# First-level scores of a gated recurrence as biased exponentials, and four reordered stage openings

## The reference

```python
# output projections, three times for the 2048 tokens (8 feature tiles in, 16 in the last)
y = jnp.concatenate([...], axis=-1) @ w_out[l]
x = x + gate[:, None, :] * y
# gated recurrence, per chunk, 4 heads of width 128
cum = jnp.cumsum(li, axis=2)
diff = cum[:, :, :, None, :] - cum[:, :, None, :, :]
decay = jnp.where(causal, jnp.exp(jnp.where(causal, diff, 0.0)), 0.0)
scores = jnp.einsum('bhtd,bhsd,bhtsd->bhts', qi, ki, decay)
```

## Time and profile before

| | us |
|---|---|
| median of 3 executions | 4637.68 |
| lowest, highest | 4636.55, 4641.71 |
| profiled execution, its own time | 4641.9 |
| its span in the trace | 4640.2 |
| mean granted clock of TensorE | 0.926 |

### The profile page before, as it was taken

How to read it: one execution, slowest core, us unless ns; L and a number is a source line. 1 busy time by engine, 2 the same in 40 slices (tenths; PEclk the granted TensorE clock), 3 DMA queues, 4 the chain that set the end, 5 groups by cost and what they waited for, 6 DMA issues and landing times. The chain is left out here.

```text
span 4640.2 us, 51312 instructions
## 1 busy us (share of the span) xinstructions
PE 3943.1 (85%) x19136; PEld 3222.7 (69%) x19136; DVE 2494.6 (54%) x3386; ACT 1577.0 (34%) x2597; POOL 1140.8 (25%) x972
## 2 busy tenths in 40 slices
PE   4659998798895999869879799999997968776998
PEld 1548887686574888668758578878885656664776
DVE  2645943687363594368736643330000489994554
ACT  2332102675211210257622212241111755553331
POOL 1421110121111111012111111111110158874443
PEclk7879999799997999889989899999998989997999
DMA  5341112322454112232246412131211465554443
GB/s 214 120 152 63 68 77 88 96 64 81 155 199 144 71 75 77 78 97 64 62 154 231 162 68 77 72 141 68 81 68 68 136 155 146 147 136 158 171 169 111
DMA packets 315680, 529.46 MB, mean 114 GB/s; under 512 B 26806, under 2 KB 203574, under 8 KB 299512
## 3 DMA queue, kind: packets, MB, share of 16 engines
q1 hardware_dynamic: 276874, 353.84, 24.6%
q0 software_dynamic: 38592, 172.82, 10.0%
HBM read 373.57 MB, written 153.00 MB: 113 GB/s over the span
## 5 line engine op out<-in xcount | busy, mean ns | idle before, releaser
L450 PE MATMUL in_ps<-h,in_wp 128*128 128x512 f32 x6624 | 1510.3, 390 | 18.6 <-POOL in_wp L613 18.6
L450 PEld LDWEIGHTS in_ps<-h,in_wp 128*128 128x128 f32 x6624 | 1247.6, 188 | 281.4 <-POOL in_wp L613 21.6
L1656 PE MATMUL out_ps<-out_y,out_wp 128*128 128x512 f32 x3072 | 728.5, 399 | 77.0 <-ACT out_y L1536 34.5
L1656 PEld LDWEIGHTS out_ps<-out_y,out_wp 128*128 128x128 f32 x3072 | 589.1, 192 | 216.3 <-issue 65.7
L583 DVE SCALAR_TENSOR_TENSOR cy<-cu,in_cw,cy 128x2048 f32<-128x2048 f32 x120 | 314.5, 2621 | 4.3
L872 PE MATMUL att_O<-att_pT,att_vs 128*128 128x512 f32 x960 | 302.8, 424 | 0.0
L1589 POOL TENSOR_TENSOR out_wp<-out_w,out_wp 128x2048 fp32r<-128x2048 f32 (+1 forms) x48 | 192.7, 4016 | 441.7 <-ACT out_wp L1525 441.6
L511 ACT ACTIVATE in_ob<-in_ps 128x2048 f32<-128x2048 f32 x37 | 69.7, 1885 | 664.1 <-PE in_ps L450 664.1
L613 POOL TENSOR_TENSOR in_wp<-in_w,in_wp 128x1024 fp32r<-128x1024 f32 x75 | 201.6, 2690 | 250.3 <-ACT in_wp L461 214.6
L992 DVE TENSOR_TENSOR att_pT<-att_T,att_pT 128x512 fp32r<-128x512 f32 x320 | 219.6, 686 | 73.8 <-ACT att_pT L925 65.7
L1918 DVE TENSOR_SCALAR hi_z<-hi_z 128x4 f32<-128x4 f32 x1 | 0.2, 172 | 462.0 <-ACT hi_z L1875 462.0
...
## 6 DMA issues: line engine op xcount, KB each, us to landing
...
```

Source lines behind the costliest of these rows:

```text
L450: mm = nc.tensor.matmul(ps[:, q, c * W:(c + 1) * W], wp[:, q, i, k], h[:, j, k, c * W:(c + 1) * W], start=(n + k == 0), stop=(n == 2 and k ...
L1656: mm = nc.tensor.matmul(ps[:, u % NB, :W], wp[:, u % NW, a, k], y[:, c % 2, b, k], start=(i + k == 0), stop=(i == 2 and k == KY - 1))
```

## The change

Four stage functions are edited.

1. `project`, only where there are decays (`in_2`): the weight parts of tiles (0,0), (0,1) and (1,0) are all made ahead of the first body, the last of them on ACT after the input heads.
2. `attention`: the queries of block 0 are loaded and rounded ahead of the second piece of keys; the rests of the first pieces stand ahead of the constants on DVE; the value parts and the later key pieces, which stood behind the eight heads of block 0, stand between them.
3. `project_out`. In `out` of the first layer: two buffers `mw`, and the unused products go to PSUM (two banks, for which the units' banks fall from 5 to 4); in both layers `gather` comes ahead of `modulation`, and each dot product waits for the one before. In `out_2`: the second weights are loaded and rounded right behind the first input piece; PE takes units 0 and 1 piece by piece (`pieces`, 12 matmuls for each piece) and no longer one after the other; in chunks 1 to 3 the squares of units 0, 1 and 2 are taken together in the place of the third.
4. `mixers`: level 0 has no differences. DVE writes the negated sum at the middle of the chunk (`edge`, 128x4), and ACT takes the exponentials straight from `hc` and `hkc` with a bias for each head: 8 of 128x64 in the place of one of 128x512. `pick(c, 0)` copies the one quarter of `psL` that level 0 fills (64 partitions by 4x64).

```diff
+        soon = decays
         def tiles(eng, body, ahead=None, only=None):
             def tile(it, q, *rest, last=False):
-                if ahead is not None and not last:
+                if ahead is not None and not last and not (soon and isinstance(it, int) and it == 0):
                     ahead(it + q, 1 - q)
                 body(rest[0], it, q, *rest[1:])
             if ahead is not None:
                 ahead(0, 0)
+                if soon:
+                    ahead(0, 1)
+                    ahead(1, 0)
...
+                if soon and isinstance(it, int) and (it, q) == (1, 0):
+                    heads()
...
-            for p in range(FIRST):
+            keys(0)
+            queries(0)
+            for p in range(1, FIRST):
                 keys(p)
...
+            def value_heads(g):
+                act.wait_ge(v_in, 32 if win else 16)
+                nc.scalar.activation(vs[:, :, 0, 2 * g * HD:(2 * g + 1) * HD], vf[:, :, g * HD:(g + 1) * HD], ACT.Copy).then_inc(vled, 1)
-            for p in range(FIRST):
-                key_heads(p)
+            key_heads(0)
             query_heads(0, 0)
             query_heads(0, 1)
+            for p in range(1, FIRST):
+                key_heads(p)
             for hh in range(NH):
                 exps(0, hh)
                 if hh < 2:
                     query_heads(1, hh)
+                elif hh < 4:
+                    value_heads(hh - 2)
+                elif FIRST + hh - 4 < len(cuts):
+                    key_heads(FIRST + hh - 4)
             sink_exps(0)
-            act.wait_ge(v_in, 32 if win else 16)
-            for g in range(2):
-                nc.scalar.activation(vs[:, :, 0, 2 * g * HD:(2 * g + 1) * HD], vf[:, :, g * HD:(g + 1) * HD], ACT.Copy).then_inc(vled, 1)
-            for p in range(FIRST, len(cuts)):
-                key_heads(p)
...
+            def value_rest(g):
+                dve.wait_ge(vled, g + 1)
+                of, to = slice(g * HD, (g + 1) * HD), slice(2 * g * HD, (2 * g + 1) * HD)
+                tt(vs[:, :, 1, to], vf[:, :, of], vs[:, :, 0, to].bitcast(F32), ALU.subtract).then_inc(vparted, 1)
+            for p in range(FIRST):
+                key_rest(p)
...
                 maxima(0, hh)
+                if 3 <= hh < 5:
+                    value_rest(hh - 3)
+                elif 5 <= hh and FIRST + hh - 5 < len(cuts):
+                    key_rest(FIRST + hh - 5)
             shift(0)
-            dve.wait_ge(vled, 2)
-            for g in range(2):
-                of, to = slice(g * HD, (g + 1) * HD), slice(2 * g * HD, (2 * g + 1) * HD)
-                tt(vs[:, :, 1, to], vf[:, :, of], vs[:, :, 0, to].bitcast(F32), ALU.subtract).then_inc(vparted, 1)
-            for p in range(FIRST, len(cuts)):
-                key_rest(p)
...
-    NB, SQ, S1, S2 = 5, 5, 6, 7
+    NB, SQ, S1, S2 = (4, 4, 5, None) if later and not middle else (5, 5, 6, 7)
...
+    FIRST, SQUARE_AT = (G, 0) if kept else (1, 2)
...
+        products = s.ps("products", [P, 2 * CH]) if later and not middle else None
...
-                wait(sp, dotted, j * m_n)
-                sp.dma_start(mw[:], m_w[j]).then_inc(mw_in, 16)
+                wait(sp, dotted, (j + 1 - NMW) * m_n)
+                sp.dma_start(mw[:, j % NMW], m_w[j]).then_inc(mw_in[j % NMW], 16)
...
-            weights(1)
+                if p + 1 == FIRST:
+                    weights(1)
...
-                square(u)
+                if kept or c == 0 or n > SQUARE_AT:
+                    square(u)
+                elif n == SQUARE_AT:
+                    for v in range(u - SQUARE_AT, u + 1):
+                        square(v)
...
+            def pieces():
+                for p in range(G):
+                    for u in range(2):
+                        for i, (a, b) in enumerate(PARTS):
+                            if p == 0 and i < 2:
+                                pe.wait_ge((led, parted)[i], u + 1)
+                            if u == 0 and i != 1:
+                                pe.wait_ge((yled, None, yparted)[i], p + 1)
+                            for k in range(p * KP, (p + 1) * KP):
+                                mm = nc.tensor.matmul(ps[:, u, :W], wp[:, u, a, k], y[:, 0, b, k], start=(i + k == 0), stop=(i == 2 and k == KY - 1))
+                        if p == G - 1:
+                            mm.then_inc(mm_done, 1)
             pe.wait_ge(const, 3 if middle else 2)
-            for u in range(U):
+            if not kept:
+                pieces()
+            for u in range(0 if kept else 2, U):
...
-                dve.wait_ge(mw_in, 16 * (j + 1))
+                dve.wait_ge(mw_in[j % NMW], 16 * (j // NMW + 1))
                 dve.wait_ge(silued, m_n)
                 for n in range(m_n):
-                    out = unused if n + 1 < m_n else mw
-                    nc.vector.tensor_tensor_reduce(out=out[:], in0=mw[:], in1=mc[:, n], scale=1.0, scalar=0.0,
+                    wait(dve, dotted, j * m_n + n)
+                    out = mw[:, j % NMW] if products is None else products[:]
+                    nc.vector.tensor_tensor_reduce(out=out, in0=mw[:, j % NMW], in1=mc[:, n], scale=1.0, scalar=0.0,
...
                 add(u)
+                gather(u)
                 if later and 0 <= u - LEAD < NJ:
                     modulation(u - LEAD)
                 if later and u - LEAD == NJ:
                     modulations_done()
-                gather(u)
...
+                    if n == 0:
+                        half = P // 2
+                        wait(act, levelled, (c - 2) * NM + 1)
+                        for h in range(H):
+                            nc.scalar.activation(X[:, q, 0, h, half:], hc[:, d, h, half:], ACT.Exp, bias=edge[:, q, h:h + 1])
+                            ins = nc.scalar.activation(X[:, q, 0, h, 0:half], hkc[:, d, h, 0:half], ACT.Exp, scale=-1.0, bias=hc[:, d, h, half - 1:half])
+                        ins.then_inc(hexpd, 1)
+                        return
...
-                    edge = cum[:, :, 0, 0, m - 1:m].broadcast_to([P, H, m])
-                    tt(x[:, :, 0, 1], cum[:, :, 0, 1], edge, sub)
-                    tt(x[:, :, 0, 0], edge, kc[:, :, 0, 0], sub).then_inc(differed, 1)
+                    wait(dve, hexpd, (c - 2) * NE + 1)
+                    ts(edge[:, q], hc[:, d, :, m - 1], -1.0, None, mul).then_inc(differed, 1)
...
+                    part = psL[0:half, 0].rearrange("p (h t) -> p h t", h=H)[:, :, half:]
+                    nc.vector.tensor_copy(S[0:half, c % 2, :, half:], part).then_inc(picked, 1)
```

28 lines of the change are left out of this document (15 added, 13 removed).

## The result

The changed kernel takes **4579.92 us** (median of 4, 4577.96 to 4585.07) against 4639.69 us for the kernel before in the same comparison: a ratio of 0.9867 with a 95% interval of 0.9844 to 0.9889. The prediction was 4556 us, with a range of 4535 to 4590. The sign was right and the time lies in the range, but of 81 us that were worked out some 60 came.

A forecast was written before the change was run, and what follows sets the result against it. The prediction took PE to bound the projections and VectorE to bound `mix`. Terms of 11.4 + 13 + 18 + 28 + 11 = 81.4 us took 4641.9 to 4560.5 us, or 4556 us after a 4.2 us median correction; range 4535 to 4590.

The forecast's parts named there:

- `in_2`: Weight projection stage: PE's wait before the third tile and the half clock behind it go, 11.4 us (8 to 12).
- first `out`: First layer's output projection: a second `mw` buffer ends VectorE's waits for loads, 18 us (12 to 20).
- chunk starts of `out_2`: In `out_2`, PE's three idle times at chunk starts and the half clock behind them go, 19.9 us.
- Attention: Both attention stages: rests moved between the eight heads save 7.3 us in the first, 5.9 in the second, together 13.
- opening of `out_2`: Start of `out_2`: units 0 and 1 taken piece by piece let PE finish them earlier, 8 us (5 to 12).
- Second `out`: Second layer's output projection: only `gather` moves ahead of the products, hidden by PE, so no gain or loss.
- Rival (b): The openings give only about two thirds, 25 us fewer, program at about 4581 us; chance 15%.
- term of 0.7 us times 15: In `mix`, two differences leave VectorE and a small edge comes in, 0.7 us a chunk, 11 us in all.
- rival (a): In `mix`, holds move to other operations or late exponentials stall GpSimd; 11 us fewer, program 4567 us; chance 25%.
- estimate of ScalarE's cover: In `mix`, ScalarE's idle 2.02 us covers 1.4 us more exponential work a chunk, leaving about 0.6 us.
- Rival (c): In `mix`, the copy's saving counts and the holds vanish, 15 us more, program 4541 us; chance 15%.
- (d): In `mix`, later GpSimd products hold VectorE's two-input operations at four more places a chunk, program 4648 us; chance 2%.

The follow-up runs named there:

- e7: The changed kernel, but in `out_2` each square stands at its own unit again, the piece-by-piece opening kept: 4595.86 us.
- e1: The changed kernel, but in the second `out` the sums (`gather`) stand behind the product with `mw` again: 4571.59 us.
- e3: The changed kernel, but `pick(c, 0)` in `mix` is the full masked copy of 128x512 again: 4576.14 us.
- e5: The kernel of e1, but in `mix` VectorE's edge no longer waits for PE's output of the chunk before: 4568.86 us.
- e9: The kernel of e5 with `gather` behind in the first `out` too, and in `mix` the edge behind `hgates` and `hupdate`: 4568.93 us.
- e12: The changed kernel with the old `mixers`, `gather` behind in both `out` stages, and ten PE matmuls ahead of the wait for the last pick: 4556.70 us.
- e10: The kernel of e5 with `gather` behind in the first `out` too, but ScalarE makes the edge instead of VectorE: 4583.34 us.

## Why the prediction was right, and where it failed

**`in_2`, first `out` and the chunk starts of `out_2`: right in mechanism and size.** Their terms were 11.4, 18 and 19.9 us, and they measured 11.3, 18.0 and 18.0. The exact 18.0 of the first `out` is luck in its last digits, as the traces of that stage spread from 198.1 to 201.7 us, a gain of 15 to 19. What they have in common is that a whole idle time of PE stood in the profile with its releaser, that the thing it waited for was moved ahead of a named blocker, and that the next candidate could be timed from rows. Charging the half clock behind each idle time was right too: e7 gives 18.0 us where its idle times alone are 12.8.

**Attention and the opening of `out_2`: right in sum, in part by luck.** The attentions were to give 13 us and gave 14.5. But in the first the moved rests gave 3.9 us for 7.3, since the estimate charged 2.8 us for what doesn't fit between the heads and the heads took 4.4 us longer; in the second they gave 5.2 for 5.9. The missing part came from the start of the stage, 2.3 and 3.2 us, which the prediction put at nothing because "the first score needs both anyhow". The first maximum stands 15.8 and 16.5 us into the stage before and 13.1 to 14.2 in all 13 traces with the new order. Whether the queries ahead of the second key piece or the key rests ahead of the constants give this, no run separates. In the opening (8.7 us for 8) the estimate counted 24 matmuls behind the last piece, 5.6 us; a piece has 12 for both units together, and PE is through with them 3.6 us after it starts on the piece (4225.36 to 4228.93). Against that the last piece reaches PE 5.8 us later in the stage than before (40.8 against 35.0 us), where 3 us were charged. The two errors cancel.

**Second `out`: the step that failed is "only `gather` moves ahead of the products, where PE already fills its window: nothing, hidden by PE itself".** It cost about 8 us, as e1 shows. The step asked whether PE is busy, not what is queued behind the new wait: VectorE's product with `mw`, and behind that the load into the only buffer and the input pieces on the same queue. PE at 97.5% of its window had no slack to hide it. The prediction named no price for the loss of that cover. Rival (b) had the openings give less together, but for other reasons.

**`mix`: the step that failed is the term of 0.7 us times 15.** The premise "what shortens VectorE's list there shortens the stage, and nothing else does" is wrong, as e3, e5 and e9 (VectorE's list changed, distance not) and e12 (list not changed, 1.0 us less) show. VectorE was 98% busy, but its busy time contained the holds by GpSimd. Taking the two operations away shortened their own stretch by 0.60 us, and 0.24 us of that came back in holds of others, so that 0.36 us stayed. The range for this term, from -5 to +25, held the result, and rival (a), "the recurrence gains nothing", is what happened; it had 25%. Its mechanism, holds that move to other operations, is one half of the cause; outputs of PE in half clock are the other, differing from trace to trace, and no rival had that. The estimate of ScalarE's cover was right: it was to idle some 0.6 us before the second exponential of `L`, and it does so for 0.66.

```profile
3876.34 0.60 ACT L2317 ACTIVATE mix_L<-mix_psB 128x512 f32<-128x512 f32 x1 [0.66 <-PE mix_psB L2647]
```

**Rival (c)**, that the removed operations take their holds along, didn't come; **(d)** neither, though e10 is its like: one more small operation on ScalarE ahead of the exponentials, and the stage is 10 us longer.
